# Two output projections of a transformer block in three passes of rounded operands, their weights split beside other work

## The reference

```python
# block 1, token_mix: mLSTM heads and HGRN heads, gated and normalised
merged = jnp.concatenate([out_m, out_h], axis=-1)      # 256 x 1024
y = merged @ w_out                                     # 1024 x 1024
h = h + g2 * rmsnorm(y, mix_post_g)                    # then the second feed-forward block

# block 2: attention and RWKV time mix, gated and added
merged = sigmoid(gate_fox) * (y_fox @ p_fox) + sigmoid(gate_rwkv) * (y_rwkv @ p_rwkv)
x = layer_norm(ALPHA * x + merged @ w_o)               # then the product-key experts
```

## Time and profile before

| | us |
|---|---|
| three runs | 1791.41, 1791.76, 1792.88 (median 1791.76) |
| the profiled execution, its own time | 1789.91 |
| its span | 1788.0 |
| PE busy | 1741.2 (97%) |
| DVE, ACT, POOL busy | 1128.5, 776.7, 348.9 |
| granted PE clock, mean | 0.996 of full speed |

### The profile page before, as it was taken

One profiled execution on the slowest core, in us unless ns is written; L12 is line 12 of the kernel. 1 busy time (PEld: TensorE's weight loads), 2 busy tenths in 40 slices (PEclk: granted clock), 3 DMA queues, 4 the chain that ended last, 5 costly groups with the idle time before them and its releaser, 6 DMA issues.

```text
span 1788.0 us, 32976 instructions
## 1 busy us (share of the span) xinstructions
PE 1741.2 (97%) x12794; PEld 1532.0 (86%) x12794; DVE 1128.5 (63%) x2022; ACT 776.7 (43%) x1229; POOL 348.9 (20%) x323
## 2 busy tenths in 40 slices
PE   6999999999999999999899999999999999999997
PEld 3999889875999899778749999999999988888886
DVE  3887557663565555974634799488899844444444
ACT  4434444653454454642124534544444443333334
POOL 2000000111000000000010676500000055555553
PEclk9999999999999999999999999999999999999999
DMA  9878554456565534430044455544444566666665
GB/s 347 288 270 285 207 205 170 141 189 224 188 211 169 192 122 142 155 128 26 26 165 145 131 175 178 164 143 145 144 145 146 154 192 195 190 196 189 195 192 165
DMA packets 64386, 314.42 MB, mean 176 GB/s; under 512 B 7152, under 2 KB 7568, under 8 KB 44688
## 3 DMA queue, kind: packets, MB, share of 16 engines
q1 hardware_dynamic: 62928, 305.94, 51.6%
q10 hardware_dynamic: 1280, 6.82, 1.0%
q0 software_dynamic: 64, 0.04, 0.0%
HBM read 311.72 MB, written 1.05 MB: 175 GB/s over the span
## 4 chain that ended last, share of the span: by engine, by line
PE 90%; DVE 4%; ACT 2%; DMA 2%; issue 1%; POOL 0%; SPq 0%; DVEq 0%; POOLq 0%; ACTq 0%
PE bank L409 24%; PE bank L410 23%; PE bank L411 23%; PE bank L698 3%; PE bank L2773 3%; PE bank L2747 1%; DMA ring<-in_stream 1%; DVE ring_rounded L371 1%; PE bank L1345 1%; PE bank L2347 1%; PE bank L775 1%; DMA ring<-in_experts 1%; PE bank L2360 1%; PE bank L1998 0%; PE bank L2012 0%
## 5 line engine op out<-in xcount | busy, mean ns | idle before, releaser
L411 PE MATMUL bank<-yb_rounded,ring_rounded 128*128 128x256 f32 x2000 | 567.3, 284 | 0.0
L411 PEld LDWEIGHTS bank<-yb_rounded,ring_rounded 128*128 128x128 f32 x2000 | 385.1, 193 | 0.0
L2864 ACT CAST ring_rounded<-ring 128x1024 fp32r<-128x1024 f32 x248 | 260.6, 1051 | 274.7 <-DMA ring<-in_experts 274.7
L371 DVE TENSOR_TENSOR ring_rounded<-ring,arena_rounded 128x1024 fp32r<-128x1024 f32 x214 | 252.0, 1220 | 128.6 <-ACT arena_rounded L360 128.4
L409 PE MATMUL bank<-yb_rounded,arena_rounded 128*128 128x256 f32 x1104 | 316.9, 287 | 1.7 <-DVE yT_rounded L891 1.3
L410 PE MATMUL bank<-yT_rounded,arena_rounded 128*128 128x256 f32 x1104 | 314.1, 285 | 0.0
L409 PE MATMUL bank<-yb_rounded,ring_rounded 128*128 128x256 f32 x960 | 278.2, 290 | 0.7 <-POOL ring_rounded L3071 0.5
L3027 DVE TENSOR_TENSOR ring_rounded<-ring,ring_rounded 128x1024 fp32r<-128x1024 f32 x128 | 156.9, 1225 | 190.6 <-ACT ring_rounded L2864 190.6
L410 PE MATMUL bank<-yT_rounded,ring_rounded 128*128 128x256 f32 x960 | 271.4, 283 | 0.0
L410 PE MATMUL bank<-ring_rounded,arena_rounded 128*128 128x512 f32 x688 | 267.7, 389 | 0.0
L360 ACT CAST arena_rounded<-ring 128x1024 fp32r<-128x1024 f32 x214 | 213.2, 1048 | 101.7 <-PE bank L409 99.5
(11 more groups left out here) (438 smaller groups left out, 2698.6 us busy)
## 6 DMA issues: line engine op xcount, KB each, us to landing
ring<-in_stream SPq DMA_DIRECT2D x144, 1024.0 KB, 4.9
ring<-in_experts SPq DMA_DIRECT2D x256, 512.0 KB, 3.5
field<-in_stream SPq DMA_DIRECT2D x24, 512.0 KB, 7.0
field<-in_stream SPq DMA_DIRECT2D x4, 1024.0 KB, 7.7
field<-in_gains ACTq DMA_DIRECT2D x3, 512.0 KB, 7.4
field<-in_gains ACTq DMA_DIRECT2D x1, 1536.0 KB, 6.2
const<-in_const SPq DMA_DIRECT2D x1, 1473.0 KB, 11.5
xh<-in_x ACTq DMA_DIRECT2D x1, 1024.0 KB, 5.6
```

Source lines behind the costliest of these rows:

```text
L371: ins = nc.vector.tensor_tensor(ring_r[:, g % SLOTS, half], ring[:, g % SLOTS, half], top.bitcast(F32), ALU.subtract)
L411: return first, pe.matmul(bank, s_rest, m_top, start=False, stop=stop)
L2864: nc.scalar.copy(expert_top[:, n % E_SLOTS, :], expert_w[:, n % E_SLOTS, :]).then_inc(expert_top_ready, 1)
```

## The change

`output_pe` multiplies in three passes: for every plain matmul it issues three, with the split activations (`y_top`, `y_rest`) on the staying side and the split chunk on the moving side. Both stages get four top slots of their own. The four chunks of each projection are cast by ACT and subtracted by DVE. For `w_out` the first chunk is split inside the loop (ACT in its turn i = 5, DVE in its turn i = 6), the other three after the turned activations. For `w_o` the first chunk is cast before the last `group_root_act` and subtracted in two halves between the last merges. PE no longer waits for all four banks to be copied; each part waits for its own quarter of `y_rest`. The scaling of the six pieces goes from ACT (six instructions of 128x128) to POOL (two of 128x384), behind the reciprocal `h_rstd`. The DMA of the layer norm's gains (`lns_in`) stands behind the three casts on ACT.

```diff
-        def output_pe(pe):
+        def output_pe(pe, stage, tag):
+            chunk_at[stage] = chunks.n
+            split_stage("pe", stage)
             four = [V.take(pe) for _ in range(4)]
             def part(w, n, t, c):
                 for k in range(4):
-                    ins = pe.matmul(four[2 * t + n][:, :], yT[:, c + k, t * P:(t + 1) * P], w[:, k, :],
-                                    start=(c + k == 0), stop=(c + k == KT - 1))
+                    first, last = three_passes(pe, four[2 * t + n][:, :], (y_top[:, t, c + k, :], y_rest[:, t, c + k, :]), w[k],
+                                               c + k == 0, c + k == KT - 1)
...
             for c in (0, 4):
-                w = chunk()
+                w = next_split_chunk(pe, 4)
                 for t in range(TT):
+                    pe.wait_ge(A.free, turned_at[tag] + 4 + 2 * t + c // 4 + 1)
...
-            w = [chunk(), chunk()]
+            w = [next_split_chunk(pe, 4), next_split_chunk(pe, 4)]
...
-            pe.wait_ge(sem("h_scaled"), 1)
+            pe.wait_ge(sem("h_scaled"), TT)
             turn_pe(pe, yb, "mixed")
-            A.evacuated(pe)
-            output_pe(pe)
+            output_pe(pe, "w_out", "mixed")
...
+                if i == last - 2:                                     # ACT, in the loop
+                    act.wait_ge(sem("gains_mixed"), 2)
+                    split_stage("act", "w_out")
+                    top_chunks.n = chunk_at["w_out"]
+                    top_chunk_act(act, 8)
...
-            act.wait_ge(sem("h_rstd"), 1)
-            for i in range(last - 1):
-                ...
-                ins = nc.scalar.activation(at, at, ACT.Copy, scale=head_rstd[:, 8 + i:9 + i])
-            ins.then_inc(sem("h_scaled"), 1)
             a(head_square(last))
...
-            turn_act(act)
+            turn_split_act(act)
+            for gap in (8, 1, 2):
+                top_chunk_act(act, gap)
+            act.wait_ge(begun, chunk_at["w_out"] + 2)
             own_top_act(act, "ffn2")
...
+            pool.wait_ge(sem("h_rstd"), 1)                            # POOL
+            heads = HEADS - 1
+            for t in range(TT):
+                y = yb[:, t, W1:W1 + heads * P].rearrange("p (h w) -> p h w", w=P)
+                rstd = head_rstd[:, 8:8 + TT * heads].rearrange("p (h t) -> p t h", t=TT)[:, t, :]
+                nc.gpsimd.tensor_tensor(y, y, rstd.unsqueeze(2).broadcast_to([P, heads, P]), ALU.mult).then_inc(sem("h_scaled"), 1)
...
+                if i == last - 1:                                     # DVE, in the loop
+                    split_stage("dve", "w_out")
+                    rest_chunks.n = chunk_at["w_out"]
+                    rest_chunk_dve(dve)
...
             take_out(last)
+            turn_split_dve(dve, turned_at["mixed"])
+            for _ in range(3):
+                rest_chunk_dve(dve)
...
             recurrence_act(act)                                       # block 2
+            split_stage("act", "w_o")
+            top_chunks.n = chunk_at["w_o"]
+            top_chunk_act(act, 4)
             group_root_act(act, ROUNDS - 1)
-            turn_act(act)
+            turn_split_act(act)
+            for _ in range(3):
+                top_chunk_act(act, 4)
...
             merge_dve(1, 0).then_inc(sem("y_merged"), 1)
+            rest_chunk_dve(dve, (0,))
             v(merge_dve(0, 1))
+            rest_chunk_dve(dve, (1,))
             merge_dve(1, 1).then_inc(sem("y_merged"), 1)
+            turn_split_dve(dve, turned_at["merged"])
+            for _ in range(3):
+                rest_chunk_dve(dve)
```

More of the change, by code:

```diff
@@ L218, in program @@
                        for name, n in [*list(shared.items())[:3], *sizes.items(), ("tiny", 512)]}
[L219 to L220 removed]
+        ring_flat_r, yT_r, yb_r, arena1_r, arena2_r, arena3_r, arena4_r, arena5_r, tiny_r = [
+            rounded[name] for name in ("ring", "yT", "yb", "arena1", "arena2", "arena3", "arena4", "arena5", "tiny")]
         ring_flat, yT_flat, yb, field, tiny = [sb(name, [P, n]) for name, n in shared.items()]
@@ L276, in program @@
             "mix2": [halves((arena2_r, 3072), (arena2_r, 4096)), halves((arena2_r, 5120), (arena4_r, 5120))],
+            "w_out": [halves((arena4_r, 1024), (arena4_r, 2048)), halves((arena2_r, 0), (arena2_r, 1024)),
+                      halves((arena5_r, 2048), (arena5_r, 3072)), halves((arena5_r, 4096), (arena5_r, 5120))],
+            "w_o": [halves((arena2_r, 3072), (arena2_r, 4096)), halves((arena2_r, 5120), (arena4_r, 5120)),
+                    halves((arena1_r, 4096), (arena1_r, 5120)), halves((arena1_r, 6144), (arena1_r, 7168))],
             "peer": [halves((arena3_r, 0), (arena3_r, 1024)), halves((arena3_r, 2048), (arena3_r, 3072))]}
@@ L289, in top_slot @@
         def top_slot(stage, i):
+            if stage in ("w_out", "w_o"):
+                return top_slots[stage][i]
             special = {("mix", 15): 3, ("ffn", FT + FT // 2 - 1): 2}
@@ L360, in top_chunk_act, with rest_chunk_dve @@
                 nc.scalar.copy(top, ring[:, g % SLOTS, half * HALF:(half + 1) * HALF]).then_inc(sem("weight_top_ready"), 1)
[L362 to L367, removed]
+        def rest_chunk_dve(dve, parts=range(2)):
+            c = weight_splits["dve"]
+            if 0 in parts:
+                rest_chunks.n += 1
+                c.n += 1
+            g = rest_chunks.n - 1
+            for i in parts:
+                top = slot_of("dve")[i]
                 half = slice(i * HALF, (i + 1) * HALF)
@@ L608, in turn_split_dve @@
                                         y_top[:, t, k:k + 4, :].bitcast(F32), ALU.subtract).then_inc(A.free, 1)
[L610 to L615, removed]
         def moving_pe(pe, queue, k_tiles=KT, src=None):
@@ L697, in part @@
                 for k in range(4):
-                    ins = pe.matmul(four[2 * t + n][:, :], yT[:, c + k, t * P:(t + 1) * P], w[:, k, :],
-                                    start=(c + k == 0), stop=(c + k == KT - 1))
+                    first, last = three_passes(pe, four[2 * t + n][:, :], (y_top[:, t, c + k, :], y_rest[:, t, c + k, :]), w[k],
+                                               c + k == 0, c + k == KT - 1)
                     if k == 0:
-                        first = ins
-                return first, ins
-            chunk = lambda: next_chunk(pe)[:, :].rearrange("p (k n) -> p k n", k=4)
+                        begins = first
+                return begins, last
             for c in (0, 4):
-                w = chunk()
+                w = next_split_chunk(pe, 4)
                 for t in range(TT):
+                    pe.wait_ge(A.free, turned_at[tag] + 4 + 2 * t + c // 4 + 1)
                     first, last = part(w, 0, t, c)
@@ L2373, in mix2_pe @@
             turn_pe(pe, yb, "merged")
-            A.evacuated(pe)
-            output_pe(pe)
+            output_pe(pe, "w_o", "merged")
             V_end["mix2"] = V.filled.n
@@ L2616, in mix2_dve @@
             merge_dve(1, 0).then_inc(sem("y_merged"), 1)
+            split_stage("dve", "w_o")
+            rest_chunks.n = chunk_at["w_o"]
+            rest_chunk_dve(dve, (0,))
             v(merge_dve(0, 1))
+            rest_chunk_dve(dve, (1,))
             merge_dve(1, 1).then_inc(sem("y_merged"), 1)
+            turn_split_dve(dve, turned_at["merged"])
+            for _ in range(3):
+                rest_chunk_dve(dve)
             first = V_end["mix2"] - 4
```

5 lines of the change are left out of this document (2 added, 3 removed).

## The result

The changed kernel takes 1780.71 us, median of 5 runs (1776.96 to 1783.17); the kernel before takes 1791.41 beside it (5 runs, 1789.11 to 1792.88). The ratio is 0.9937, 95% interval 0.9921 to 0.9954: 10.7 us less in the medians, where 11.65 was forecast. The profiled spans are 1778.9 and 1788.0, 9.1 us apart; the forecast of the span was 1776.3.

A forecast was written before the change was run, and what follows sets the result against it. PE, busy 97% of the span, was taken to bound the kernel. w_out -6.05 and w_o -5.6 made -11.65 us, from 1791.76 to 1780.1 us; range 1777.5 to 1784.5.

The forecast's parts named there:

- The passes: On PE in both projections: 96 passes at 0.229 us take 22.0 us, saving 5.7 at w_out, 5.6 at w_o.
- Three quarters of the old stage: Rival for both projections: passes at 0.215 us, 2.6 us less in all, 1777.5 us; chance 0.06.
- The loop: w_out's first chunk split inside the loop: about 0.15 us reaches PE, bounds 0 and 1.0.
- The start: Start of w_out on PE: 404.3 instead of 405.82, -1.5 us, bounds -2.0 and 0.
- Chunk 3: Middle of w_out: lands after 6.4 us, split by 414.5, needed 415.3; cost 0.2 us, bounds 0 and 1.6.
- the prediction's own sign of being wrong: In its list of signs: the forecast is wrong if PE waits over 1 us for chunk 3.
- The cover: Behind w_out: matmuls covering t = 0's chain shrink from 6.9 to 5.5 us; +0.95 us, bounds 0 and 1.2.
- `w_o`: Second projection: -5.6 us, all from the passes; its start and shorter cover taken as 0.
- DVE against POOL: Rival around w_out: the two engines block each other, one block of 1.1 and one of 2.3 us; 1783.5 us, chance 0.06.
- longer stages behind: Sign of a wrong forecast: the stages behind (ffn2, the experts) take longer than before.

The follow-up runs named there:

- e4_late_wait: Changed kernel, but PE waits for chunk 3's split only ahead of the matmuls that read it, in both projections; 1777.89 us, ratio 0.994.
- e10_first_behind_filled: Changed kernel with w_out's first chunk split behind the loop and 18 small matmuls of constants in PE's wait for it; 1783.84 us, ratio 0.9955.
- e7_first_chunk_behind: Changed kernel with w_out's first chunk cast and subtracted behind the loop instead of inside it; 1784.7 us, ratio 0.9962.
- e1_only_w_out: Changed kernel with w_o put back as before (plain matmuls, ScalarE copies, no splits); 1785.19 us, ratio 0.9967.
- e3_scale_on_act: Changed kernel with the six pieces scaled by ACT again instead of POOL; 1780.62 us, ratio 0.9943.
- e5_six_more_passes: Changed kernel with six idle 128x512 passes added in w_out between the second half's t = 0 and t = 1 parts; 1778.46 us, ratio 0.9926.
- e8_late_wait_and_square: Changed kernel with PE's later wait for chunk 3 and ACT's square of t = 1's first half ahead of t = 0's chain; 1777.75 us, ratio 0.9923.
- e6_two_passes: Changed kernel with the pass on the activations' rest left out in both projections, all splits still made, result not the reference's; 1776.6 us, ratio 0.9911.
- e9_gains_later: Changed kernel with the gains' 1.5 MB transfer placed in ACT's program after the second of three groups of casts; 1780.53 us, ratio 0.9936.
- e11_gains_behind_casts: Changed kernel with the gains' transfer issued by ACT behind all three groups of casts; 1778.34 us, ratio 0.9932.
- e12_all_three: Changed kernel with PE's later wait for chunk 3, the earlier square on ACT, and the gains issued behind all casts; 1777.68 us, ratio 0.993.
- e2_only_w_o: Changed kernel with w_out put back to plain matmuls and ScalarE copies, POOL's scaling kept; 1784.74 us, ratio 0.9961.

## Why the prediction was right

The mechanism was right: less time on PE, an earlier start, and a part given back at chunk 3 and at the cover. The stages give 11.66 us less by the local distances, against 11.65 forecast, and that close a match is luck: `w_out` gave 0.47 less than its 6.05, `w_o` 0.48 more than its 5.6.

- **The passes.** 0.229 apart, as in the earlier trace rows; 22.1 us of `w_out` without its gap, 21.9 of `w_o`. Three quarters of the old stage, the prediction's estimate from the Trainium skill (FP8 and Floating Point Precision, TensorE Precision Notes), would have been 20.7, which the measured 0.229 a pass doesn't give.
- **The loop.** Forecast 0.15, measured 0.00: the stretch is 8.68 in both. On ACT it went as forecast. With the 1.05 by which this trace is ahead, the copy stands at 392.2 instead of 391.34, 0.9 late, but nothing of it came to PE. DVE's three products for turn 7 ended 0.50 ahead of `attend(7)` before and end 0.19 ahead of it now, so most of the reserve is used up:

```profile
389.28 1.99 ACT L366 CAST arena_rounded<-ring 128x1024 fp32r<-128x1024 f32 x2 [1.32 <-issue]
391.18 0.58 ACT L798 COPY field<-bank 128x512 f32<-128x512 f32 x1
```

- **The start.** -1.5 forecast, -1.85 measured: the turns began where the forecast had them (401.85 on the clock of before, forecast 401.95), and the first pass came 2.12 behind them, not 2.35. POOL's two scalings took what was expected and end at 399.5, before L1699 whose piece PE waits for last:

```profile
397.86 1.62 POOL L1558 TENSOR_TENSOR yb<-yb,small 128x384 f32<-128x384 f32 x2 [13.83 <-DVE small L1718]
```

- **Chunk 3: the term that was mis-sized.** Forecast 0.2, measured 1.0 from pass to pass (1.1 by `e4_late_wait`). That is at the edge of the prediction's own sign of being wrong, a wait of over 1 us for chunk 3; the wait that the trace shows is 0.85. The step that failed is "with 6.4 us it lands at 411.2": it was issued at 403.42 and landed 7.9 later. The 6.4 of the earlier trace rows was read with the gains' transfer already 3.9 us on its way; in the changed kernel it had a lead of 2.4. Over the kernels, lead and landing of this chunk:

| gains issued ahead of the chunk by | landing of the chunk |
|---|---|
| 6.8, 7.1 us (`e10_first_behind_filled`, `e7_first_chunk_behind`) | 4.8, 5.0 |
| 3.9 (before) | 6.4 |
| 2.4 (changed, `e1_only_w_out`, `e3_scale_on_act`, `e4_late_wait`, `e5_six_more_passes`, `e8_late_wait_and_square`) | 7.9 to 8.0 |
| 2.4 (`e6_two_passes`) | 6.7 |
| -0.1 (`e9_gains_later`) | 8.8 |
| issued after it landed (`e11_gains_behind_casts`, `e12_all_three`) | 5.0, 4.8 |

`e11_gains_behind_casts` moves nothing but the gains, so 3 of the 7.9 us are the neighbour's. In the first row the gains had landed, 6.2 to 6.3 us after their issue, when the chunk was issued. I had the direction ("the gains' transfer now overlaps it longer") and took almost nothing for it. `e6_two_passes` stands aside from the order by 1.2 us; why is open, and so a lead alone doesn't give the landing.

- **The cover.** +0.95 forecast, +0.84 measured (1.06 of waiting against 0.22), confirmed from both sides: a longer cover brings the wait to 0.21 (`e5_six_more_passes`), the old one to 0.22 (`e2_only_w_o`).
- **`w_o`.** -5.6 forecast, -6.08 measured: 5.70 from the passes, and 0.38 from the start. First pass after the last merges at 10.18 instead of 10.56; I had taken 0, because t = 1's turn held the start. It did, but the old `w_o` also waited for all four copies: the last of them ended at 906.58 and the first matmul started at 906.64. With its plain matmuls `e1_only_w_out` has the old 10.55, `e2_only_w_o` the new 10.18.
- **DVE against POOL.** The rival's mechanism happened, off the path. DVE's L1728 beside POOL's two subtractions for `ffn2`:

```profile
415.94 3.31 DVE L1728 SCALAR_TENSOR_TENSOR field<-field 128x1024 f32<-128x1024 f32 x1
```

```profile
415.00 6.50 POOL L408 TENSOR_TENSOR arena_rounded<-field,arena_rounded 128x1024 fp32r<-128x1024 f32 x2 [15.52 <-ACT arena_rounded L400]
```

DVE's took 1.23 in `e11_gains_behind_casts` (above), where the two are apart, and POOL's pair 4.66 before. What was already under way went on at its own pace, and what came later was held: in the changed kernel DVE's L928 (414.69 to 415.91) took its 1.22 although POOL's first subtraction began at 415.00, and L1728 ended 1.1 behind the end of that subtraction (418.17); in `e9_gains_later` DVE's instruction began first (417.81) and took 1.23, while POOL's pair, begun at 418.25, took 5.41. Beside the scaling on POOL (397.86 to 399.48) DVE's two mask instructions, which read a PSUM bank, took 0.65 and 0.74, as before (0.65 and 0.73). POOL ended at 421.50 and the chain's first instruction on DVE (L495 of t = 0) came at 422.12, so PE saw none of it. The forecast had POOL done before that instruction; it was, with 0.6 to spare.

Outside the two stages the profiled changed kernel had 1.05 us less up to `attend(7)` (396.17 against 397.22) and 3.6 more behind: 457.05 against 455.46 from `ffn2` to the last merges, 851.2 against 849.2 in the experts. I named longer stages behind as something that would make the forecast wrong. The change doesn't force them: behind the last turn `e4_late_wait`, with both stages changed, takes the 849.2 of the kernel before and of `e2_only_w_o`. But the other kernels with `w_out` changed lie between 849.9 and 853.1 (`e6_two_passes` at 855.1), and with one trace a kernel it isn't shown whether the change makes a longer time there more likely; the whole times, 10.7 us less with an interval of over 5 us, can't tell.

## What to carry to other kernels

When an engine at 97% sheds work, look at each thing it used to wait for or cover just in time: here the last chunk's transfer and a chain of small operations on ACT gave back 1.9 of some 13.5 us. A transfer's duration read from a trace holds only for the same neighbours at the same lead; take the longest landing on record as the bound, or let PE ask for one chunk at a time. And read edits worth a us from local distances in the trace, since whole runs of this kernel can't resolve them.

## What the runs showed of the hardware

- A 1 MB load on SP's queue took 4.8 to 5.0 us where a 1.5 MB transfer on ACT's queue had landed or wasn't yet issued, and 8.8 where that was issued 0.1 us behind it (`e9_gains_later`).
- ACT's transfer was issued at 404.53 although four casts ahead of it in the program ran until 408.4 (`e9_gains_later`); behind the wait for chunk 3 it was held until 408.72 (`e11_gains_behind_casts`).
- After 4.26 us of idling PE ran ten passes at the 1.2 GHz level (granted clock 0.50), at a further cost of 2.2 us (`e7_first_chunk_behind`); after 2.75 us of idling it didn't (`e6_two_passes`); multiplying constants through the wait avoided it (`e10_first_behind_filled`).
- DVE reading SBUF and POOL held each other up, the later one waiting: 1.23 became 3.31 us on DVE and 4.66 became 6.50 us for POOL's pair. DVE instructions that read a PSUM bank lost nothing beside POOL's scaling (0.65 and 0.74 us).
